# The one-step sampled sequences of two token mixers, woven between the triangular-inverse levels of the prompt tiles

## The reference, cut to what matters

```python
h = rmsnorm(x, lp['norm_g'])
proj = h @ lp['w_in']        # 1024 -> 9352 columns, split among all of these
qkv_a, z_a, beta_raw, alpha_raw, f_b, z_b, qkv_c, z_c, gate_raw = jnp.split(proj, offs, axis=-1)
...
o_a, dn_s_new = gated_delta_chunked(q_a, k_a, v_a, g_a, beta, dn_s)      # mixer A
y_b, rw_s_new = rwkv7_scan(r_h, heads(logw), k_h, v_h, -kk, kk * a_h, rw_s)  # mixer B
o_c = moba_attention(q_c, pos, k_all, v_all).reshape(B, L, W_BRANCH) * jax.nn.silu(z_c)  # mixer C
o = jnp.stack([o_a, o_b, o_c], axis=2)
up = jnp.einsum('blnc,ncd->blnd', o, lp['w_branch'])
gates = jax.nn.sigmoid(gate_raw + lp['b_gate']).reshape(B, L, N_BRANCH, D_MODEL)
x = x + jnp.sum(gates * up, axis=2) @ lp['w_out']
x = x + jax.nn.sigmoid(x @ lp['w_pg'] + lp['b_pg']) * (ple @ lp['w_ple'])
```

## Time and profile before

| | |
|---|---|
| median of 3 runs | 1184.14 us (1183.62 to 1186.87) |
| the profiled execution, its time | 1179.26 us |
| the profiled execution, its span from first to last instruction | 1177.0 us |
| PE (TensorE matmul) busy | 1139.6 us, 97% |
| DVE (VectorE) busy | 570.0 us, 48% |
| ACT (ScalarE) busy | 323.7 us, 27% |
| POOL (GpSimd) busy | 131.7 us, 11% |
| chain that ended last | 89% PE, of which line 1150 alone 63% |
| mean granted TensorE clock | 0.975 of full speed |

### The profile page before, as it was taken

One profiled execution on the slowest core, in us unless ns is written; L12 is line 12 of the kernel. 1 busy time (PEld: TensorE's weight loads), 2 busy tenths in 40 slices (PEclk: granted clock), 3 DMA queues, 4 the chain that ended last, 5 costly groups with the idle time before them and its releaser, 6 DMA issues.

```text
span 1177.0 us, 20908 instructions
## 1 busy us (share of the span) xinstructions
PE 1139.6 (97%) x8148; PEld 871.2 (74%) x8148; DVE 570.0 (48%) x1251; ACT 323.7 (27%) x718; POOL 131.7 (11%) x215
## 2 busy tenths in 40 slices
PE   7999999999899999999999999999998999999998
PEld 5777877778678687777767778777775877777776
DVE  4576466755735605221245764756566454161212
ACT  2243213312413243300123332233133132433001
POOL 0212041020111100000001120501102011000000
PEclk9999999999959999999999999999997899999999
DMA  6833136413303775364237322543232067453621
GB/s 217 250 108 114 55 109 198 125 39 97 86 2 117 202 221 176 90 212 146 74 113 209 113 77 89 163 142 91 72 98 50 19 210 199 153 157 108 218 83 41
DMA packets 168654, 148.44 MB, mean 126 GB/s; under 512 B 41705, under 2 KB 157007, under 8 KB 168365
## 3 DMA queue, kind: packets, MB, share of 16 engines
q1 hardware_dynamic: 164167, 136.65, 39.4%
q0 software_dynamic: 2848, 7.79, 1.9%
q10 hardware_dynamic: 1541, 2.66, 0.7%
HBM read 135.42 MB, written 11.07 MB: 124 GB/s over the span
## 4 chain that ended last, share of the span: by engine, by line
PE 89%; DVE 4%; ACT 2%; SPq 2%; DMA 2%; issue 1%; POOL 0%; ACTq 0%; DVEq 0%; POOLq 0%
PE psum L1150 63%; PE psum L1075 4%; PE psum L1343 2%; PE psum L1326 2%; PE psum L1200 1%; PE psum L1457 1%; PE psum L1718 1%; PE psum L1554 1%; PE psum L1564 1%; PE psum L1338 1%; PE psum L1323 1%; ACT arena L1785 1%; PE psum L1697 1%; SPq L976 1%; PE psum L1578 1%
## 5 line engine op out<-in xcount | busy, mean ns | idle before, releaser
L1150 PE MATMUL psum<-x_b,ring 128*128 128x288 f32 x1296 | 343.0, 415 | 1.7 <-DMA ring<-in_w_in 1.7
L1150 PE MATMUL psum<-x_a,ring 128*128 128x288 f32 x1296 | 340.2, 413 | 0.5 <-DVE x_a L2246 0.5
L1150 PEld LDWEIGHTS psum<-x_b,ring 128*128 128x128 f32 x1296 | 241.2, 192 | 71.3 <-issue 8.2
L1150 PEld LDWEIGHTS psum<-x_a,ring 128*128 128x128 f32 x1296 | 239.3, 191 | 68.9 <-issue 8.7
L1785 ACT ACTIVATE arena<-psum 128x512 f32<-128x512 f32 (+5 forms) x150 | 67.2, 472 | 182.9 <-PE psum L1075 68.9
L1150 PE MATMUL psum<-z,ring 128*128 128x288 f32 x384 | 99.7, 409 | 0.0
L1150 PEld LDWEIGHTS psum<-z,ring 128*128 128x128 f32 x384 | 70.6, 190 | 17.9 <-issue 0.7
L1150 PE MATMUL psum<-merged,ring 128*128 128x288 f32 x256 | 62.4, 406 | 0.0
L1785 ACT ACTIVATE arena<-arena 128x256 f32<-128x256 f32 (+9 forms) x102 | 44.5, 464 | 64.1 <-DVE arena L2833 28.7
L1075 PE MATMUL psum<-consts,arena 128*128 128x128 f32 (+2 forms) x362 | 53.2, 279 | 6.2 <-DMA arena<-in_x_prompt 4.6
L1150 PEld LDWEIGHTS psum<-merged,ring 128*128 128x128 f32 x256 | 48.6, 190 | 13.4
(11 more groups left out here) (404 smaller groups left out, 1430.1 us busy)
## 6 DMA issues: line engine op xcount, KB each, us to landing
ring<-in_w_in SPq DMA_DIRECT2D x72, 1024.0 KB, 5.3
ring<-in_w_branch SPq DMA_DIRECT2D x24, 512.0 KB, 3.6
arena<-in_cache_k SPq DMA_DIRECT2D x32, 256.0 KB, 3.1
arena<-in_cache_v SPq DMA_DIRECT2D x32, 256.0 KB, 3.2
ring<-in_w_out SPq DMA_DIRECT2D x8, 1024.0 KB, 6.3
ring<-in_w_pg SPq DMA_DIRECT2D x8, 1024.0 KB, 5.1
arena<-in_state_dn SPq DMA_DIRECT2D x8, 512.0 KB, 8.0
out_dn_sample<-arena POOLq DMA_DIRECT2D x8, 512.0 KB, 6.5
```

Of the source, the lines that this page charges most:

```text
L1150: ins = mm(out[:, 0:NTOK], lhs, rhs(k), **flags)
```

## The change

The sampled-tile steps of A move between `lev_y` and `lev` of unit 0, those of B between `lev_y` and `lev` of units 1 and 2. `as_out` and `bs_out` stay behind the levels. `bs_out` is done in two halves (pair 0, pair 1), each with its own VectorE masking, product, addition, decay and turn. The sampled tile's output norm comes ahead of that of tile 0. Since both run at the same time now, the sampled steps get buffers and PSUM regions of their own (M[2], M[3], M[4] instead of M[0] and M[1], the buffers `AKQ`, `AR`, `BBK`, `BY` and a third row of the sums), and the waits of PE follow these. `b_fin`, which stores the prompt's final state, comes ahead of tile 1's norm. `FILL` is written anew for the whole layer; the number of pieces is the same.

Pieces between the first `lev_y` of a unit and `b_w` of tile 1 (`a_w` in unit 0), as the two lists give them:

| stretch | before | after |
|---|---|---|
| unit 0 | 36 | 47 |
| unit 1 | 23 | 23 |
| unit 2 | 9 | 24 |

In unit 2, step by step, ahead of each step after the first `lev_y`: before 0 lev, 0 lev_y, 0 lev, 0 lev_y, 1 lev, 0 lev_y, 0 lev, 1 lev_y, 0 lev, 0 lev_y, 1 lev, 2 b_u, 4 b_w. After: 2 lev, 2 lev_y, (bs_pairs) 0 lev, 3 lev_y, (bs_in, bs_sq) 1 lev, 5 lev_y, (bs_s0, bs_inv, bs_w) 0 lev, 2 lev_y, (bs_u) 3 bs_y, 0 lev, (b_w) 0 lev_y, 2 lev, 1 b_u, 3 b_norm5 of t = 2, 0 b_w. In unit 1 after: 1 lev, 1 lev_y, (bs_pairs) 1 lev, 1 lev_y, 2 lev, 3 lev_y, 0 lev, 2 lev_y, 4 bs_y, 0 lev, 0 lev_y, 1 lev, 2 b_u, 5 b_norm5, 0 b_w.

```diff
-    def both_tiles(u):
+    def both_tiles(u, beside={}):
 
         for k in range(1, NLEV):
             if k == NLEV - 1 and u:
                 add("b_w", u - 1, 0)
             add("lev_y", u, k)
+            for s in beside.get(k, ()):
+                add(*s)
             add("lev", u, k)
 
...
-    both_tiles(0)
+    both_tiles(0, {1: [("as_scale",)], 2: [("as_pairs",)], 3: [("as_sq",), ("as_inv",)], 4: [("as_s0",), ("as_w",)],
+                   5: [("as_u",), ("as_o",)], 6: [("a_norm2", 2)]})
     add("a_u", 0)
+    add("a_norm3", 2)
+    add("a_norm4", 2)
     add("a_o", 0)
+    add("a_norm5", 2)
     add("a_w", 1)
     add("a_norm2", 0)
+    add("a_norm6", 2)
     add("a_u", 1)
     add("a_norm3", 0)
     add("a_norm4", 0)
     add("a_o", 1)
     add("a_norm2", 1)
     add("a_norm5", 0)
-    add("as_scale")
     add("a_norm3", 1)
     add("a_norm4", 1)
     add("a_norm6", 0)
-    add("as_pairs")
     add("a_norm5", 1)
-    add("as_sq")
+    add("as_out", 0)
     add("a_norm6", 1)
-    add("as_s0")
-    add("as_inv")
-    add("as_w")
-    add("as_u")
-    add("as_o")
-    add("as_out", 0)
-    add("a_norm2", 2)
-    add("a_norm3", 2)
-    add("a_norm4", 2)
     add("as_out", 1)
-    add("a_norm5", 2)
-    add("a_norm6", 2)
     add("b_hist")
     add("b_lora", 0)
     add("b_lora", 1)
...
-        both_tiles(1 + g)
+        add("bs_nat", g)
+        both_tiles(1 + g, {1: [("bs_scale", g)], 2: [("bs_pairs", g)], 3: [("bs_in", g), ("bs_sq", g)],
+                           4: [("bs_s0", g), ("bs_inv", g), ("bs_w", g)], 5: [("bs_u", g), ("bs_y", g)],
+                           6: [("b_norm1", g, 2), ("b_norm2", g, 2)]})
         add("b_u", g, 0)
+        add("b_norm3", g, 2)
+        add("b_norm4", g, 2)
         add("b_y", g, 0)
+        add("b_norm5", g, 2)
         add("b_norm1", g, 0)
         add("b_w", g, 1)
+        add("b_norm6", g, 2)
         add("b_norm2", g, 0)
         add("b_u", g, 1)
+        add("bs_out", g, 0)
         add("b_norm3", g, 0)
         add("b_norm4", g, 0)
+        if g == 0:
+            add("b_exp", 1, 0)
         add("b_y", g, 1)
         add("b_norm1", g, 1)
         add("b_norm5", g, 0)
-        add("bs_nat", g)
         add("b_norm6", g, 0)
+        add("b_fin", g)
         add("b_norm2", g, 1)
-        add("bs_scale", g)
-        if g == 0:
-            add("b_exp", 1, 0)
+        add("bs_out", g, 1)
+        add("bs_store", g)
         add("b_norm3", g, 1)
         add("b_norm4", g, 1)
-        add("bs_pairs", g)
-        add("bs_in", g)
         add("b_norm5", g, 1)
-        add("bs_sq", g)
         add("b_norm6", g, 1)
         if g == 1:
             add("c_fetch_k", 0)
             add("c_fetch_k", 1)
-        add("bs_s0", g)
-        add("bs_w", g)
-        add("bs_inv", g)
-        add("bs_u", g)
-        add("bs_y", g)
-        add("b_norm1", g, 2)
-        add("b_fin", g)
-        add("b_norm2", g, 2)
-        add("bs_out", g)
-        add("b_norm3", g, 2)
-        add("b_norm4", g, 2)
-        add("b_norm5", g, 2)
-        add("b_norm6", g, 2)
-        add("bs_store", g)
...
-FILL = [0, 0, 32, 12, 3, 24, 13, 0, 11, 0, 6, 0, 2, 6, 6, 1, 3, 12, 0, 4, 0, 2, 16, 1, 2, 2, 2, 3, 2, 2, 2, 2, 2, 2,
...
+FILL = [0, 0, 40, 19, 2, 2, 22, 1, 7, 0, 6, 0, 12, 1, 4, 4, 0, 12, 1, 3, 0, 2, 15, 2, 0, 2, 0, 4, 5, 0, 1, 4, 0, 1, 0,
...
             def as_scale(l):
                 pe.wait_ge(S.sem("a_unit"), S.count("a_unit"))
-                pe.wait_ge(S.sem("a_state"), S.count("a_state"))
-                pe.wait_ge(S.sem("a_nat"), S.count("a_nat"))
+                pe.wait_ge(S.sem("a_lt"), S.count("a_lt"))
                 for i in range(2):
                     r = slice(32 * i, 32 * i + 4)
-                    mm(M[i][:, 0:128], C("ones")[r], ASX[r], start=True, stop=True)
-                mm(M[0][:, 128:129], ASX[0:4], C("ones")[0:4, 0:1], start=True, stop=True).then_inc(S.sem("a_gb"), 1)
...
-            def bs_out(l, g):
+            def bs_out(l, g, pr):
                 pe.wait_ge(S.sem("b_bex"), S.count("b_bex"))
                 pe.wait_ge(S.sem("b_nats"), S.count("b_nats"))
-                for pr in range(2):
-                    for hh in range(2):
-                        r, o = rows_of(half_of(hh, pr)), rows_of(hh)
-                        ins = mm(M[pr][o, :], BN[r, pr, 0, o], BX[r, pr, :, :], start=True, stop=True)
+                if pr == 0:
+                    pe.wait_ge(S.sem("b_done"), S.count("b_done"))
+                for hh in range(2):
+                    r, o = rows_of(half_of(hh, pr)), rows_of(hh)
+                    ins = mm(M[0][o, :], BSKN[r, pr, o], BX[r, pr, :, :], start=True, stop=True)
                 ins.then_inc(S.sem("b_ds"), 1)
 
...
             def b_y(l, g, t):
                 w = wid(t)
+                if t == 0:
+                    pe.wait_ge(S.sem("b_ys"), S.count("b_ys", pos[("bs_y", l, g)]))
...
             def b_norm5(l, g, t):
-                pe.wait_ge(S.sem("b_nats"), S.count("b_nats"))
-                pe.wait_ge(S.sem("b_ws"), S.count("b_ws"))
                 pe.wait_ge(S.sem("out_normed"), S.count("out_normed"))
                 if t == 2:
+                    pe.wait_ge(S.sem("tri_up"), S.count("tri_up"))
+                    ins = tr(M[0][:, 0:128], BYB)
+                else:
+                    pe.wait_ge(S.sem("b_nats"), S.count("b_nats"))
+                    pe.wait_ge(S.sem("b_ws"), S.count("b_ws"))
                     pe.wait_ge(S.sem("b_fin_s"), S.count("b_fin_s"))
-                    ins = tr(M[4][:, 0:128], BYB)
-                else:
                     for pr in range(2):
...
-            def bs_out(l, g):
-                link(tt(BUV, BSU, BSV, ADD))
-                tt(BX, bc(BUV.rearrange("p (q n) -> p q n", q=2), 2, [128, 2, NSEQ, 64]),
-                   C("own8").unsqueeze(1).unsqueeze(3).to_broadcast([128, 2, NSEQ, 64]), MUL).then_inc(S.sem("b_bex"), 1)
+            def bs_out(l, g, pr):
+                tt(BX[:, pr], bc(BUV[:, 64 * pr:64 * pr + 64], 1, [128, NSEQ, 64]), bc(C("own8"), 2, [128, NSEQ, 64]), MUL).then_inc(S.sem("b_bex"), 1)
                 dve.wait_ge(S.sem("b_bex"), S.count("b_bex"))
                 dve.wait_ge(S.sem("b_ds"), S.count("b_ds"))
-                flat = BSK.rearrange("p q s n -> p q (s n)")
-                link(tt(flat, flat, PS[:, 3:5, :], ADD))
-                link(tt(BSK, BSK, bc(BM[:, 2 * g:2 * g + 2, 4:12], 3, [128, 2, NSEQ, 64]), MUL))
-                dve.transpose(BSN.rearrange("p q s n -> p (q s n)"), BSK.rearrange("p q s n -> p (q s n)")).then_inc(S.sem("b_snew"), 1)
+                new, old = (b[:, pr].rearrange("p s n -> p (s n)") for b in (BSK, BSN))
+                link(tt(new, new, M[0], ADD))
```

More of the change, by code:

```diff
@@ L686, in program @@
         AEG, AGB, ADI, AKB, AVB, AKD = (part(4, 128) for _ in range(6))
-        AKQ = part(1024)
+        AKQ = part(8, 128)
         AVN, AKN, AQK, AW, AU, AST, AR = (part(4, 128) for _ in range(7))
@@ L694, in program @@
         AGC = part(3, 4)
-        ASM = part(2, 4)
+        ASM = part(3, 4)
         ASQ = [arena[:, a:a + 4 * NTOK].rearrange("p (h n) -> p h n", h=4) for a in (7552, 7552 + 1536)]
@@ L703, in program @@
         flat = lambda b: b.rearrange("p h n -> p (h n)")
-        ASE = AEG
+        ASE = AKQ[:, 0:4, :]
         ASB, ASV, ASKF, ASK = AKBF[:, 0:128], flat(AVB)[:, 0:128], flat(AVB)[:, 128:256], flat(AKD)[:, 0:128]
         ASL, ASA, AST1, ASQ2 = (ADI[:, i, :] for i in range(4))
-        ASQK, ASTT = AQK[:, 0, :], AQK[:, 1, :]
-        ASVN, ASKN = AVN[:, 0, :], AVN[:, 1, :]
-        ASW, ASO, ASU, ASX = AW[:, 0, :], AW[:, 1, :], AU[:, 0, :], AR[:, 1, :]
+        ASQK, ASTT, ASVN, ASKN = (AKQ[:, i, :] for i in range(4, 8))
+        ASU, ASX, ASW, ASO = (AR[:, i, :] for i in range(4))
         SECOND_A = [LTA, LOA, heads(AGBF, 0, 64), heads(AGBF, 256, 64), TTA]
@@ L849, in program @@
         a_squares = lambda t: (AKN, AKN1, AKBF[:, 128:256].unsqueeze(1))[t]
-        a_sums = lambda t, i: ASM[:, i, 0:1] if t == 2 else ASM[:, i, :]
+        b_sums = lambda t, i: BSM[:, 2, i:i + 1] if t == 2 else BSM[:, i, :]
+        a_sums = lambda t, i: ASM[:, 2, i:i + 1] if t == 2 else ASM[:, i, :]
         ident = C("ident")
@@ L1348, in as_s0 @@
                 pe.wait_ge(S.sem("a_scaled"), S.count("a_scaled"))
+                pe.wait_ge(S.sem("a_nat"), S.count("a_nat"))
                 for s in range(NSEQ):
@@ L1357, in as_u @@
                 pe.wait_ge(S.sem("a_w"), S.count("a_w"))
-                pe.wait_ge(S.sem("tri_ys"), S.count("tri_ys"))
-                mm(M[1][:, 0:128], ASTT, ASW, start=True, stop=True).then_inc(S.sem("corrected"), 1)
+                pe.wait_ge(S.sem("tri_ys"), S.count("tri_ys", pos[("as_inv", l)]))
+                mm(M[4][:, 0:128], ASTT, ASW, start=True, stop=True).then_inc(S.sem("corrected"), 1)
             def as_o(l):
@@ L1400, in a_o @@
                 pe.wait_ge(S.sem("corrected_s"), S.count("corrected_s"))
+                if t == 0:
```

(21 more changed lines are left out.)

96 lines of the change are left out of this document (53 added, 43 removed), and 12 rows, old and new, of the table FILL.

## The result

| | before | after |
|---|---|---|
| median | 1185.24 us (4 runs, 1183.62 to 1186.87) | 1171.82 us (4 runs, 1171.23 to 1172.17) |
| profiled execution, time and span | 1179.26 and 1177.0 us | 1172.17 and 1170.4 us |
| granted clock, mean of the profiled one | 0.975 | 0.995 |

The ratio is 0.9886, with a 95% interval of 0.9869 to 0.9903: 13.4 us faster. The forecast was 1151 us with a range of 1143 to 1167, so the direction was right and the size was not: 13.4 us in place of 33. From profiled execution to profiled execution the step is 7 us only.

What follows compares the result with a forecast made beforehand. PE bounds the kernel by its instructions' time, its waits and its low clock. Terms -29.8 + 3 - 6.6 = -33.4 us on the profiled 1179.3 give 1145.9, as a median 1151 us; range 1143 to 1167.

Steps and rivals of the forecast that it cites:

- Unit 2, -29.8 us: Unit 2, both layers: with 24 pieces for 9 it costs what unit 1 did, 29.8 us less.
- The clock: Unit 2's clock, 0.59 and 0.64 before, rises to full; below 1.0 in any unit would show the prediction wrong.
- VectorE's order, +3 us: Units 0 to 2: sampled steps queue ahead of the levels' subtractions on VectorE; +3 us, bounds 0 to 30.
- GpSimd beside the levels: Unit 0, levels 4 to 6: subtractions and turns free beside GpSimd's decays; by plain port sharing some 5 us a layer.
- Elsewhere. 0: Stretches outside the units run full at full clock, so giving up cover there costs 0, bounds -3 and +15 us.
- Longer waits in mixer C: A listed sign that the prediction is wrong: PE waiting longer in mixer C; no size given.
- The rival on missing cover: Tail and mixer C's steps lack the 15 moved pieces a layer: at most 14.6 us back, 1165 us; chance 0.06.
- The rival on SyncE's queue: State load of g = 1 behind g = 0's stores comes late at bs_in: slower, 1188 us; chance 0.05.
- The halves of bs_out, 0: Split instructions at bs_out: four more on VectorE for each g, off PE's path, 0 us.
- The waits behind the units, -6.6 us: PE's waits at as_out, bs_out, the last sampled norm and b_lora all go: -6.6 us, bounds 0 to -6.6.
- The median, +4.9 us: The runs' median lies 4.9 us above the profiled execution before; the same difference was added to the forecast.

Runs made afterwards that it cites:

- e2: The kernel before with only FILL changed: 15 pieces go from the tail and tiles to unit 2's level steps, no step moved; 1168.17 us, ratio 0.9887.
- e1: The kernel after with the last state store (bs_store of g = 1) placed behind c_fetch_k; 1161.55 us, ratio 0.9818.
- e6: The kernel before with only FILL changed: unit 2's 15 more pieces taken from the tail of g = 1; 1196.49 us, ratio 1.0111.
- e9: e1 plus 6 pieces in unit 1 and 4 behind unit 2, from the 15 ahead of b_norm3 and b_norm4; three side fillers put back; 1163.43 us.
- e11: e1 with 6 more pieces in unit 1, taken from the 57 ahead of b_lora; 1166.14 us.
- e4: The kernel after with bs_out in one step again, at the place of the second half; 1173.08 us.
- e5: e1 with the halves of bs_out cut by sequence, not by pair, the first half moved directly ahead of b_y of tile 1; 1162.51 us.
- e7: The kernel before with mixer A's part of the change alone, B's steps and pieces as they were; 1178.62 us, ratio 0.9971.

## Why the prediction was wrong

- **Unit 2, -29.8 us: right.** e2 has -28.3 with the pieces alone. In the kernel after the two stretches are 19.8 us shorter without their records (20.7 and 21.0 us, where before has 32.7 and 28.9), with 8.0 us of sampled products moved in: 27.8. The -28.3 holds the part up to `c_past`, thinner cover behind unit 2 and all.
- **The clock: right in the units, wrong behind them.** It is 1.00 in every unit. A low stretch of 6.8 and one of 3.4 us came in mixer C.
- **VectorE's order, +3 us: right.** Without records and sampled products (3.8 us) unit 1 takes 16.2 us for 15.9, unit 2 16.7 and 17.0. That is 2.5 us for both layers. `bs_in` never waits for the state.
- **GpSimd beside the levels: right for the level steps.** In the kernel after the decays run from 131.51 to 139.55, beside levels 4 and 5 of unit 0. The subtractions in there (one input in PSUM) take the 0.69 us that they take elsewhere. The masking, now clear of the decays, takes 0.65 us apiece for 1.8 before. What the prediction didn't list is a `z_silu` that falls in there (two inputs in SBUF): it takes 2.17 us, and 0.76 us where GpSimd is idle, so VectorE loses 1.4 us a layer.

```profile
132.07 0.69 DVE L2498 TENSOR_TENSOR triangles<-triangles,psum 128x512 f32<-128x512 f32 x1 [0.35 <-PE psum L1330]
135.60 2.17 DVE L2263 SCALAR_TENSOR_TENSOR z<-tanh_z,z 128x576 f32<-128x576 f32 x1
167.20 1.29 DVE L2449 TENSOR_TENSOR arena<-arena,consts 128x512 f32<-128x512 f32 x2
```

- **"Elsewhere. 0": this is the step that failed.** The stretches outside ran full, and I read from that that they had room. The row on which it rested shows that PE is busy, not by how much each partner's chain (VectorE's, ScalarE's, a DMA's) is early. The prediction never asked where the new order puts `bs_store` on SyncE's queue: it goes from behind the copies of `c_sq` (398.66 and 387.57 before) to ahead of them (365.77 and 380.52). e1 prices this at 10 us by the medians, 8 by the ratios, and 12 us by the profiles, with the low clock behind the wait in it. e2, e6, e9 and e11 lost at four more places by taking their cover or shifting their order. "Longer waits in mixer C" was on the list of what would show it wrong, and it is what showed it.
- **The rival on missing cover** had nearly the size (14.6 us back) and not the cause. It is not the tail's steps that lack cover, but one filler that waits for DMAs with all of VectorE's work behind it. **The rival on SyncE's queue** had the right queue and the wrong transfers: the weight loads and the copies behind the store of g = 1 are late, not the state's load behind that of g = 0.
- **The halves of bs_out, 0: wrong, +4.0 us** of PE's time, though e4 and e5 show that it can't be had back.
- **The waits behind the units, -6.6 us: half.** Those at `as_out` and `b_lora` went (e7). At `bs_out` and the sampled norm they were 1.4 + 2.1 us and are 1.3 + 1.6, and tile 1's norm has a new one of 1.3 us (the rows of lines 2692, 2788 and 2790 above).
- **The median, +4.9 us: should not have been carried over.** The runs of before went from 1177 to 1193 us, with mean clocks of 0.968 to 0.980, mostly the lower clock with the longer time, and the profiled one was among the short ones. In the kernel after the profiled one (1172.17) is 0.3 us above the median. So 6 of the 13.4 us between the medians are this difference and no part of the sum, and it is luck that they bring the median nearer to the forecast: the sum is 26.8 us off, the median 20.8. Where the spread comes from stays open. The four runs of after lie within 1 us, but the six of e1, with a mean clock of 0.997 and more, spread over 5 us, and those of e2 over 13.

On the profiled executions the forecast was 26.8 us off (33.4 - 6.6). Unit 2 to `c_past` has 19.1 of it: the new wait 12.0, `bs_out` 2.0, unit 2 itself 1.9, waits behind it 2.2, and 1.0 that I cannot place. Unit 1 to unit 2 has 3.5, of which `bs_out` is 2.0. The part ahead of unit 1 has 2.0, where `bs_nat` takes 0.27 us with waits of 0.31 and 0.09 around it. The starts have 3.3, which is the scatter told above, the rest 0.3, and unit 0 gives 1.4 back.

## What to carry to other kernels

A stretch without waits is not a stretch with slack. Before taking cover from it or shifting its order, follow each partner's chain (VectorE, ScalarE, the DMA queue) through it and note by how much it is early.

When work is cut into numbered fillers, list what in them is not plain work: a copy that waits for a DMA, a table load, a tanh. A changed count shifts these past other steps, and one that waits holds its whole engine.

Price the cover and the moved steps apart. Here one list of numbers, with no step moved, was worth as much as the whole change, until one misplaced store was put right.

## What the runs showed of the hardware

- Four 64x64 products of 512 columns on four tiles take 1.0 us of PE, and so do two on two tiles.
- Four DMA copies of 72 KB, issued right behind four weight loads (DMA share 1.09 and 1.13), had VectorE waiting until 13.7 us after the first issue; where these loads had landed 3.8 to 6.5 us earlier (share 0.90 and 0.69) it was 8.5 us.
- The lower clock came with a single wait between stretches of full work (3.4 us of it with one of 4.1 us, 6.8 us with one of 5.5 us), and not only behind rows of short gaps as in unit 2.
- While GpSimd decays the state for 8.0 us, VectorE's subtraction with one input in PSUM takes its usual 0.69 us, and a `z_silu` product of 128x576 with both inputs in SBUF takes 2.17 us for 0.76.
